# Last layer norm of a two-block transformer kernel: the first token tile by ScalarE and GpSimd in column halves, the second tile scaled and stored by column halves

## The reference

```python
def layer_norm_2(x, g, b):
    xf = x.astype(jnp.float32)
    mu = jnp.mean(xf, -1, keepdims=True)
    var = jnp.mean(jnp.square(xf - mu), -1, keepdims=True)
    ...                       # (xf - mu) * rsqrt(var + eps) * g + b
        else:
            y = moe_ffn(u, moe_router[j], moe_w13[j], moe_w2[j])
        x = layer_norm_2(DEEPNORM_ALPHA * x + (1.0 + g_f) * y, ln_ffn_g[i], ln_ffn_b[i])
    return x
```

## Time and profile before

| what | value |
|---|---|
| median of three runs | 2339.42 us |
| profiled execution | 2341.7 us |
| its span, first to last instruction | 2339.8 us |
| PE busy | 2289.1 us, 98% of the span |
| DVE busy | 1838.1 us, 79% |
| ACT busy | 1324.4 us, 57% |
| POOL busy | 182.1 us, 8% |
| chain that ended last | PE 90%, DVE 6%, ACT 2% |
| last PE instruction ends | 2326.6 us |

### The profile page before, as it was taken

One profiled execution on the slowest core, in us unless ns is written; L12 is line 12 of the kernel. 1 busy time (PEld: TensorE's weight loads), 2 busy tenths in 40 slices (PEclk: granted clock), 3 DMA queues, 4 the chain that ended last, 5 costly groups with the idle time before them and its releaser, 6 DMA issues.

```text
span 2339.8 us, 33403 instructions
## 1 busy us (share of the span) xinstructions
PE 2289.1 (98%) x13171; PEld 1904.3 (81%) x13171; DVE 1838.1 (79%) x2035; ACT 1324.4 (57%) x1401; POOL 182.1 (8%) x211
## 2 busy tenths in 40 slices
PE   9999999999999999999999998999999999999997
PEld 7888778888889788889778886678888888888875
DVE  6876678777866778778685568868998989899988
ACT  5434544334434644444544347657878777778774
POOL 1101001000101001000010005400000000000010
PEclk9999999999999999999999997899999999999999
DMA  9764558657755286644145443258999999999995
GB/s 374 274 251 155 163 141 320 254 208 288 258 193 182 109 289 258 244 171 145 73 180 196 173 153 118 74 217 344 388 382 375 379 371 387 380 380 375 376 397 210
DMA packets 117478, 596.89 MB, mean 255 GB/s; under 512 B 29096, under 2 KB 29934, under 8 KB 58734
## 3 DMA queue, kind: packets, MB, share of 16 engines
q1 hardware_dynamic: 96628, 521.10, 58.2%
q0 software_dynamic: 20304, 73.98, 9.1%
q10 hardware_dynamic: 428, 0.15, 0.0%
HBM read 589.38 MB, written 5.78 MB: 254 GB/s over the span
## 4 chain that ended last, share of the span: by engine, by line
PE 90%; DVE 6%; ACT 2%; issue 1%; DMA 0%; ACTq 0%; POOL 0%; DVEq 0%; SPq 0%
PE psum L1007 20%; PE psum L1008 19%; PE psum L1060 13%; PE psum L1182 6%; PE psum L1076 3%; PE psum L1660 2%; PE psum L3355 2%; PE psum L1199 2%; PE psum L1000 1%; PE psum L1002 1%; PE psum L1001 1%; PE psum L2442 1%; PE psum L2445 1%; PE psum L2443 1%; PE psum L2550 1%
## 5 line engine op out<-in xcount | busy, mean ns | idle before, releaser
L1295 DVE TENSOR_TENSOR ring_r<-ring,ring_r 128x2048 fp32r<-128x2048 f32 x285 | 650.0, 2288 | 173.8 <-ACT ring_r L1282 173.6
L1282 ACT CAST ring_r<-ring 128x2048 fp32r<-128x2048 f32 x285 | 544.7, 1912 | 376.6 <-PE psum L1060 206.5
L1295 DVE TENSOR_TENSOR ring_r<-ring,tail_r 128x2048 fp32r<-128x2048 f32 x143 | 327.3, 2289 | 91.1 <-ACT tail_r L1282 90.9
L1282 ACT CAST tail_r<-ring 128x2048 fp32r<-128x2048 f32 x143 | 273.3, 1911 | 141.7 <-PE psum L1060 69.4
L1007 PE MATMUL psum<-ring_r,arena_r 128*128 128x512 f32 (+1 forms) x872 | 334.4, 386 | 2.0 <-DVE arena_r L1382 2.0
L1008 PE MATMUL psum<-ring_r,arena_r 128*128 128x512 f32 (+1 forms) x872 | 330.5, 382 | 0.0
L1007 PE MATMUL psum<-ring_r,xT_r 128*128 128x512 f32 (+1 forms) x576 | 215.8, 380 | 1.6 <-ACT ring_r L1280 1.6
L1008 PE MATMUL psum<-ring_r,z_r 128*128 128x512 f32 (+1 forms) x576 | 212.7, 375 | 0.0
L1060 PE MATMUL psum<-ring_r,z_r 128*128 128x512 f32 (+1 forms) x856 | 192.8, 369 | 0.0
L1007 PEld LDWEIGHTS psum<-ring_r,arena_r 128*128 128x128 f32 x872 | 164.0, 188 | 33.7 <-DVE arena_r L1382 3.2
L1008 PEld LDWEIGHTS psum<-ring_r,arena_r 128*128 128x128 f32 x872 | 164.1, 188 | 30.5
(11 more groups left out here) (610 smaller groups left out, 3839.8 us busy)
## 6 DMA issues: line engine op xcount, KB each, us to landing
ring<-in_expert_halves SPq DMA_DIRECT2D x264, 1024.0 KB, 6.7
ring<-in_dense_halves SPq DMA_DIRECT2D x165, 1024.0 KB, 7.0
arena<-in_ada_w POOLq DMA_DIRECT2D x48, 1024.0 KB, 9.5
ring<-in_mlstm_w_in SPq DMA_DIRECT2D x8, 2048.0 KB, 8.7
ring<-in_mix_out SPq DMA_DIRECT2D x4, 2048.0 KB, 7.9
ring<-in_glu_panels SPq DMA_DIRECT2D x4, 2048.0 KB, 8.9
ring<-in_mlstm_w_out SPq DMA_DIRECT2D x3, 2048.0 KB, 12.5
ring<-in_mix_in_q SPq DMA_DIRECT2D x4, 1024.0 KB, 5.0
```

Source lines behind the costliest of these rows:

```text
L1282: act.copy(upper[i % UPPERS], place(PN[r.key, i])).then_inc(upper_ready, 1)
L1295: dve.tensor_tensor(low, raw, upper[i % UPPERS], ALU.subtract).then_inc(lower_ready, 1)
```

## The change

Tile 0 of the last norm no longer goes through `center` and `scale` on the DVE. In its place:

1. The DVE writes the negated mean (`minus_mean`, one column) and, one `added` later, `rstd` of tile 0, and tells ACT of each (`mean_negated`, `rstd_ready`).
2. ACT, for each half of 512 columns: adds the negated mean, waits for itself and for `rstd`, multiplies by `rstd` (`first_scaled`).
3. POOL multiplies the left, then the right half by the gain (`left_gained`, `right_gained`), then adds the bias to the left half (`left_done`).
4. The DVE adds the bias to the right half, after `center(1)` and ahead of `scale(1)`, once `right_gained` is there.

Tile 1 keeps its `center`; its scaling is cut in two halves of 512 columns. SP stores four halves of 256 KB: right and left of tile 0, then left and right of tile 1, each after its semaphore. In the path that isn't taken the new semaphores are set by hand.

```diff
+    minus_mean = sb("minus_mean", [P, 1])
...
-        for t in range(NT):
-            ln_act(act, 9, t)
+        ln_act(act, 9, 0)
+        act.wait_ge(mean_negated, 1)
+        for half in range(2):
+            cols = slice(half * CHUNK, (half + 1) * CHUNK)
+            act.activation(z[:, 0, cols], z[:, 0, cols], ACT.Identity, bias=minus_mean[:, 0:1]).then_inc(column_done, 1)
+            act.wait_ge(column_done, half + 1)
+            act.wait_ge(rstd_ready, 1)
+            act.mul(z[:, 0, cols], z[:, 0, cols], rstd[:, 0:1]).then_inc(first_scaled, 1)
+        ln_act(act, 9, 1)
+
+    def last_pool(pool):
+
+        left, right = slice(0, CHUNK), slice(CHUNK, D)
+        pool.wait_ge(lnp_landed, lnp_count(9))
+        pool.wait_ge(first_scaled, 1)
+        pool.tensor_tensor(z[:, 0, left], z[:, 0, left], lnp[:, 0, left], ALU.mult).then_inc(left_gained, 1)
+        pool.wait_ge(first_scaled, 2)
+        pool.tensor_tensor(z[:, 0, right], z[:, 0, right], lnp[:, 0, right], ALU.mult).then_inc(right_gained, 1)
+        pool.wait_ge(left_gained, 1)
+        pool.tensor_tensor(x[:, 0, left], z[:, 0, left], lnp[:, 1, left], ALU.add).then_inc(left_done, 1)
...
         def scale(t):
-            dve.wait_ge(std_ready, NT * 9 + t + 1)
-            link(dve.reciprocal(rstd[:, t:t + 1], std[:, t:t + 1]))
-            dve.scalar_tensor_tensor(x[:, t, :], z[:, t, :], rstd[:, t:t + 1], lnp[:, 1, :], ALU.mult, ALU.add)\
-               .then_inc(x_ready, 1)
+            link(root(t))
+            for half in range(2):
+                cols = slice(half * CHUNK, (half + 1) * CHUNK)
+                dve.scalar_tensor_tensor(x[:, t, cols], z[:, t, cols], rstd[:, t:t + 1], lnp[:, 1, cols], ALU.mult, ALU.add)\
+                   .then_inc(columns_out, 1)
...
         spread_of(0)
+        dve.wait_ge(var_ready, NT * 9 + 1)
+        dve.tensor_scalar(minus_mean[:, :], mv[:, 0, 0:1], -1.0, None, ALU.mult).then_inc(mean_negated, 1)
         added(1, 0)
-        center(0)
+        root(0).then_inc(rstd_ready, 1)
         measured(1, 0)
-        scale(0)
         added(1, 1)
         measured(1, 1)
         spread_of(1)
         center(1)
+        right = slice(CHUNK, D)
+        dve.wait_ge(right_gained, 1)
+        dve.tensor_tensor(x[:, 0, right], z[:, 0, right], lnp[:, 1, right], ALU.add).then_inc(columns_out, 1)
         scale(1)
...
         for t in range(NT):
-            sp.wait_ge(x_ready, NT * 9 + t + 1)
-            sp.dma_start(out[0, t * P:(t + 1) * P, :], x[:, t, :]).then_inc(out_stored, 16)
-        sp.wait_ge(out_stored, 16 * NT)
+            for half in (1, 0) if t == 0 else (0, 1):
+                cols = slice(half * CHUNK, (half + 1) * CHUNK)
+                sp.wait_ge(*((left_done, 1) if (t, half) == (0, 0) else (columns_out, {(0, 1): 1, (1, 0): 2, (1, 1): 3}[t, half])))
+                sp.dma_start(out[0, t * P:(t + 1) * P, cols], x[:, t, cols]).then_inc(out_stored, 16)
+        sp.wait_ge(out_stored, 16 * 2 * NT)
```

More of the change, by code:

```diff
@@ L349, in program @@
     out_stored = sem("out_stored")
+    mean_negated, first_scaled, column_done = sem("mean_negated"), sem("first_scaled"), sem("column_done")
+    left_gained, left_done, right_gained = sem("left_gained"), sem("left_done"), sem("right_gained")
+    columns_out, rstd_ready = sem("columns_out"), sem("rstd_ready")
+    minus_mean = sb("minus_mean", [P, 1])
     NPARAM, NMIX, NSECOND = [0], [0], [0]
@@ L3687, in center, with root @@
                .then_inc(*step.one())
+        def root(t):
+            dve.wait_ge(std_ready, NT * 9 + t + 1)
+            return dve.reciprocal(rstd[:, t:t + 1], std[:, t:t + 1])
         def scale(t):
-            dve.wait_ge(std_ready, NT * 9 + t + 1)
-            link(dve.reciprocal(rstd[:, t:t + 1], std[:, t:t + 1]))
-            dve.scalar_tensor_tensor(x[:, t, :], z[:, t, :], rstd[:, t:t + 1], lnp[:, 1, :], ALU.mult, ALU.add)\
-               .then_inc(x_ready, 1)
+            link(root(t))
[3 more added lines that the diff above has]
+                   .then_inc(columns_out, 1)
         for half in range(2):
@@ L3795, in _ @@
                     sums_pool(pool)
+                    last_pool(pool)
     @block.scalar
@@ L3975, in _ @@
                     ln_dve(dve, step, 9, lambda t: y_sum[:, t, :], [(moe_added, EXPERTS + 1)] * NT)
+                    dve.wait_ge(x_ready, NT * 9 + NT)
+                    dve.memset(minus_mean[:, :], 0.0).then_inc(columns_out, 3)
+                    dve.memset(minus_mean[:, :], 0.0).then_inc(left_done, 1)
     @block.tensor
```

## The result

| | before | changed | changed / before |
|---|---|---|---|
| median, first comparison (12 runs each) | 2339.38 us | 2343.61 us | 1.0015 [1.0008, 1.0022] |
| the same kernel, second comparison (33 and 11 runs) | 2340.16 | 2343.20 | 1.0009 [1.0000, 1.0019] |
| third comparison (23 and 11 runs) | 2340.94 | 2342.49 | 1.0006 [0.9998, 1.0015] |
| profiled execution, its span | 2341.7, 2339.8 | 2343.25, 2341.0 | |

The changed kernel is slower, by 0.06% to 0.15% depending on which runs are asked (the third interval just includes no difference). That is under the 0.2% that was set as the bound, so "no change" came out, but the median of the first comparison, 2343.61, lies outside the range of 2337.0 to 2341.8. Two questions follow: what the last norm and the stores did, and where the rest comes from.

A forecast was written before the change was run, and what follows sets the result against it. The DVE alone was taken to set the end: 2.19 us gained, 2.97 given back, DVE 0.8 later; with queued stores the span grows 0.6, laid on 2339.42 for a median of 2340.0 us, range 2337.0 to 2341.8.

The forecast's parts named there:

- The DVE's row up to the centering: Last norm, DVE: without tile 0's two operations of 1.20 us, tile 1's centering is due at 2331.88, 2.19 us earlier.
- The lock and the turns: Last norm: DVE operations with two SBUF operands and POOL's wait out each other's whole operation, alternating; 2.97 us given back.
- The race: Tile 1's centering on DVE against POOL's right gain: whichever starts first, decides over 0.12 us only.
- The first rival: Last norm: no lock for these operations, so the end comes 1.6 us less, median 2337.8; chance 13%.
- The second: Rival, last norm: lock also takes one-SBUF-operand DVE operations, so statistics wait; slower by about 1.3 us, median 2340.7; 5%.
- The third: Rival, last norm: GpSimd slow to start on arithmetic, delaying the left gain; at 5 us the median is 2345; 2%.
- The stores: Kernel end: four queued 256 KB stores take 2.74 us without a gap, to 2339.59; plus 0.84, span 2340.4.
- the change is laid on both: Whole kernel: the 0.6 us added to the span is added to profiled 2341.7 and median 2339.42, giving 2342.3 and 2340.0.
- about 0.8 us of spread between runs on either side: Whole kernel: run spread set around the forecast's own range of 2339.5 to 2340.6 us.
- something outside the last norm moves: Rival, ahead of the last norm: the program's new layout shifts time there, either way; chance 2%.

The follow-up runs named there:

- e4: Changed kernel, with ACT copying gain and bias to PSUM, where the DVE's centering, scaling and right addition read them; end 17.4 us after norm start, ratio to before 1.0000.
- e7: Changed kernel with two whole-tile stores of 512 KB in place of four halves; end 19.4 us after norm start, ratio to before 1.0002.

## Why the prediction was right or wrong

- *The DVE's row up to the centering*: due 2331.88, came 2331.69, of which 0.08 is that the whole norm began that much earlier in this trace. The negated mean costs 0.07 to the next start, not 0.12, and the reciprocal 0.08. Right.
- *ACT* 0.71 to 0.72 each, *POOL* 1.26 alone and by the records 0.08 to 0.16 behind its releaser: right (start to start 1.22, in the earlier trace rows's stage too, where the prediction had 1.24).
- *The lock and the turns*: right in every piece. The race went to POOL although both are recorded within 0.01 us; centering 2.36 (expected "near 2.4"), POOL's addition 2.24 ("about 2.3"), the DVE's 1.75 ("over 1.5"). All three traces of the changed kernel have these to 0.01 us. The end of the scaling was expected 0.8 us later than before's and is 0.6 later; 0.1 of that comes from the first step, the rest from rounding 2335.93 up to 2336.0 and from spacings.
- *The first rival* (no lock for these operations) would have shown undisturbed durations: it fell. The second (one SBUF operand is enough) fell by the statistics, 0.69 beside POOL's 1.26. The third (a cold GpSimd) fell by the left gain, 1.26.
- *The stores*: "Data from 2336.85; four times 256 KB at 383 GB/s ... to 2339.59". Data came from 2336.6 to 2339.5 on 15 engines, near what was worked out, but on one until 2340.2. This is a step that failed: 2.74 us were set for the data, 3.6 were measured, because the sum took 16 engines for one pipe, and the end is that of the slowest engine. With the DVE 0.2 early, the end comes 0.7 later than forecast (19.4 behind the start of the norm, against 18.7).
- *The step that took the median out of the range* is the last one: "the change is laid on both", on 2339.42 from three runs of before, with "about 0.8 us of spread between runs on either side", taken from three runs within 1.57 us, and 2% for "something outside the last norm moves" because "the instructions ahead are the same". The instructions were the same and the time was not. 103 runs of before spread over 10.9 us, with a standard deviation of 2.5 and a mean of 2340.6, 1.2 above the base. Laying the change on both also put the time outside the span at no change, without a reason; it grew by 0.4.

Added up: forecast 2340.0, stores 0.7, outside the span 0.4, base 1.2, together 2342.3; measured 2343.6. Of the 1.3 left, 0.4 is that the first twelve runs of the changed kernel lie above the mean of all its 34, and 0.9 stays open, as above.

So the mechanism on the DVE and its price were right (forecast 0.8 later, measured 0.6), the stores' term was too small by 0.7, and the range was too narrow. The two corrected terms alone, 2341.1, would still have been inside it; what carried the median out is the base and the spread, and how far the runs of one comparison happened to lie apart was chance. A sign of it stood in the profile: a granted clock of 0.81 in one stage can come out otherwise in the next execution.

## What to carry to other kernels

Before work goes from DVE to GpSimd, list for each piece of it which DVE operations run beside it with two SBUF operands; each meeting costs the one that waits nearly the length of the other's operation (here 1.0 to 1.1 us beside 1.26 and 1.28), so 2.3 us saved on the DVE became 0.6 us lost. An operand in a free PSUM bank, copied by an idle ACT, took the DVE out of the conflict without changing its row (e4); at the end of the kernel that gave 0.7 us against before, too little to show in the runs. For a microsecond at the end of a kernel of 2340, compare traces from a common instruction on, and take the spread of the runs from many runs or from the clock's row, never from three.

## What the runs showed of the hardware that was not expected

- Where a packet of program code lies among the data of the stores, one of the 16 DMA engines ends 0.6 to 0.7 us behind the others, and the store with it (seven traces of seven, none of the five others). That the packet does it is inferred.
- The time of a run outside its first and last instruction is a mark of the build: 1.84 us before, 2.25 in the changed kernel, with no overlap between 91 and 34 runs.
- Of a DVE and a POOL operation that take turns, recorded within 0.01 us of each other, POOL's went first in every trace of the changed kernel and in e7, though the DVE's is the one recorded earlier. Behind POOL's end the DVE's 1024 columns took 1.09 us and its 512 columns 0.56; behind the DVE's end POOL's 512 took 1.11.
- The duration of the last norm and the stores repeats to 0.03 us between executions, while the 2320 us in front of it vary by several microseconds and go with the clock that TensorE is granted.
